# A hybrid decoder step on one core: the side loads of each head group issued by GpSimd's queue in place of SyncE's

## What is computed

```
for i in range(DEPTH):                                  # 2 layers
    h = rmsnorm(x, norm_pre)
    proj = h @ w_in                                     # 2048 -> 11296 columns, split among three branches
    y_ssd = ssd(...)     # depthwise conv4, chunked state scan with a carried state, gate, grouped norm
    y_att = swa(...)     # 128-wide sliding window attention, rotary keys, cached keys and values, sinks
    y_sc  = bg * conv3(cg * hh) * silu(g)
    x = x + rmsnorm(concat(y_ssd, y_att, y_sc) @ w_out, norm_post)
    x = x + sigmoid(x @ ple_gate) * (p[i] @ ple_proj)
# outputs: x, and per layer the conv tails, the ssd states, and the keys and values of the last 128 positions
```

## Time and profile before

| | |
|---|---|
| median of 3 runs | 2282.45 us (2279.03 to 2284.47) |
| the profiled execution | 2280.01 us, span 2278.1 us |
| PE busy | 2124.9 us, 93% |
| DVE busy | 1404.6 us, 62% |
| ACT busy | 1092.2 us, 48% |
| POOL busy | 53.8 us, 2% |
| transfers of SP and ACT (q1, q10) | 366.04 MB, 50.2% of 16 engines |
| transfers of POOL (q0) | 2.36 MB, 0.2% |
| mean granted clock of PE | 0.972 |

### The profile page before, as it was taken

How to read it: one execution, slowest core, us unless ns; L and a number is a source line. 1 busy time by engine, 2 the same in 40 slices (tenths; PEclk the granted TensorE clock), 3 DMA queues, 4 the chain that set the end, 5 groups by cost and what they waited for, 6 DMA issues and landing times.

```text
span 2278.1 us, 39608 instructions
## 1 busy us (share of the span) xinstructions
PE 2124.9 (93%) x15750; PEld 2059.2 (90%) x15750; DVE 1404.6 (62%) x2345; ACT 1092.2 (48%) x2151; POOL 53.8 (2%) x141
## 2 busy tenths in 40 slices
PE   4799999999999989998978999999999998999899
PEld 3799899899899989998967998998998997999899
DVE  4466767767766663437563666667667677534464
ACT  4456346446445443444443564564463465334443
POOL 0000000000001000000000000000000000000000
PEclk9899999999999999999988999999999999999999
DMA  5645545455365455543536455455454454555444
GB/s 174 185 140 178 161 163 175 147 181 178 118 204 169 134 179 177 176 160 123 164 131 180 140 168 192 139 170 194 142 176 156 168 177 135 173 183 175 136 141 151
DMA packets 146369, 370.94 MB, mean 163 GB/s; under 512 B 28584, under 2 KB 65256, under 8 KB 144744
## 3 DMA queue, kind: packets, MB, share of 16 engines
q1 hardware_dynamic: 133552, 336.39, 46.4%
q10 hardware_dynamic: 12488, 29.65, 3.8%
q0 software_dynamic: 144, 2.36, 0.2%
HBM read 340.41 MB, written 32.01 MB: 163 GB/s over the span
## 4 chain that ended last, share of the span: by engine, by line
PE 85%; DVE 7%; DVEq 3%; ACT 2%; issue 2%; DMA 1%; SPq 1%; ACTq 0%
PE main L426 25%; PE main L428 25%; PE main L427 24%; PE yo L545 2%; DVE wlo L1055 2%; PE yb L538 1%; DVE conv_sum L1262 1%; DVEq L1382 1%; ACT whi L723 1%; DVE work L1383 1%; PE yo L543 1%; PE t L619 1%; DVE mix L1421 1%; DVE y_or_x L1424 1%; DVEq L1422 0%
## 5 line engine op out<-in xcount | busy, mean ns | idle before, releaser
L426 PE MATMUL main<-h_hi,whi 128*128 128x288 f32 x4032 | 1223.7, 303 | 67.2 <-DVE h_lo L1055 21.7
L427 PE MATMUL main<-h_lo,whi 128*128 128x288 f32 x4032 | 1204.0, 299 | 0.0
L428 PE MATMUL main<-h_hi,wlo 128*128 128x288 f32 x4032 | 1199.9, 298 | 0.0
L1055 DVE TENSOR_TENSOR wlo<-raw,whi 128x1024 fp32r<-128x1024 f32 x568 | 690.8, 1222 | 491.9 <-ACT whi L723 478.9
L426 PEld LDWEIGHTS main<-h_hi,whi 128*128 128x128 f32 x4032 | 770.5, 191 | 87.8 <-issue 38.0
L427 PEld LDWEIGHTS main<-h_lo,whi 128*128 128x128 f32 x4032 | 772.3, 192 | 3.5 <-issue 1.9
L428 PEld LDWEIGHTS main<-h_hi,wlo 128*128 128x128 f32 x4032 | 773.2, 192 | 0.0
L723 ACT ACTIVATE whi<-raw 128x1024 fp32r<-128x1024 f32 x568 | 576.3, 1051 | 321.1 <-PE main L428 157.2
L1262 DVE SCALAR_TENSOR_TENSOR conv_sum<-conv_in,gpar_sb,conv_sum 128x312 f32<-128x312 f32 x144 | 90.1, 626 | 119.3 <-ACT conv_sum L872 111.3
L428 PE MATMUL main<-yssd_hi,wlo 128*128 128x288 f32 x512 | 152.5, 298 | 0.0
L426 PE MATMUL main<-yssd_hi,whi 128*128 128x288 f32 x512 | 151.2, 295 | 0.0
(11 more groups left out here) (239 smaller groups left out, 1702.8 us busy)
## 6 DMA issues: line engine op xcount, KB each, us to landing
raw<-wts SPq DMA_DIRECT2D x568, 512.0 KB, 3.7
work<-s_t SPq DMA_DIRECT2D x32, 512.0 KB, 5.9
ssm_s<-work ACTq DMA_DIRECT2D x8, 2048.0 KB, 7.2
work<-masks SPq DMA_DIRECT2D x8, 720.0 KB, 6.6
y_or_x<-xs SPq DMA_DIRECT2D x16, 288.0 KB, 4.2
xs<-y_or_x ACTq DMA_DIRECT2D x2, 2016.0 KB, 7.4
y_or_x<-x SPq DMA_DIRECT2D x4, 576.0 KB, 5.9
xs<-y_or_x POOLq DMA_DIRECT2D x1, 2304.0 KB, 7.8
```

The lines of the kernel that those rows point to most:

```text
L426: mm(out, w_hi, x_hi_, start=start, stop=False)
L427: mm(out, w_hi, x_lo_, start=False, stop=False)
L428: return mm(out, w_lo, x_hi_, start=False, stop=stop)
L1055: return tt(dst, raw, hi.bitcast(F32), ALU.subtract)
```

## The change

All of these side loads move from `@block.sync` to `@block.gpsimd`, with the same waits, the same order among themselves and the same semaphores. In POOL's program the first set stands at k = 0, the second at k = 1, and the four quarters of the old states at k = 14 to 17, which is behind `BM3` and ahead of the copies at k = 20. SP keeps the weights and the loads outside of the groups.

```
@@ @block.sync, for g, for k
                         load_unit(gunit(L, g, k))
-                        if k == 3:
-                            sp.wait_ge(smp_state, it(L, g))
...
-                            sp.dma_start(MSK, masks).then_inc(msk_in, 16)
-                        if k == 4:
-                            sp.wait_ge(ssd_done, it(L, g))
...
-                        if 15 <= k < 19:
...
@@ @block.gpsimd, for g, for k
+                        if k == 0:
+                            pool.wait_ge(smp_state, it(L, g))
+                            if L + g > 0:
+                                pool.wait_ge(y_sq, it(L, g - 1, 3, 2))
+                            pool.wait_ge(s1_stored, L * (G * 16) + g * 16 + 16)
+                            pool.wait_ge(k_stored, L * 32 + 32)
+                            pool.wait_ge(v_stored, L * 128 + 128)
+                            for r in range(2):
+                                pool.dma_start(KCUR[64 * r:64 * r + 64, :], kout[L, g]).then_inc(att_in, 16)
...
+                            pool.dma_start(VCUR[0:NSM, 2, :], v_g[NPR:T]).then_inc(att_in, 16)
+                            pool.dma_start(MSK, masks).then_inc(msk_in, 16)
+                        if k == 1:
+                            pool.wait_ge(ssd_done, it(L, g))
+                            pool.wait_ge(conv_saved, L * (G * 6) + g * 6 + 2)
...
+                        if 14 <= k < 18:
+                            i = k - 14
+                            if i == 0:
+                                pool.wait_ge(att_done, it(L, g))
+                            pool.dma_start(S0T...[:, :, i * P:(i + 1) * P], s0_t...).then_inc(st_in[i], 16)
                         if 8 <= k < 14:
```

More of the change, by code:

```diff
@@ L1487, in _ @@
                     for k in range(GRP_U):
+                        if k == 0:
[7 more added lines that the diff above has]
+                                pool.dma_start(KCUR[64 * r:64 * r + 64, :], kout[L, g]).then_inc(att_in, 16)
+                            pool.dma_start(KC[0:64, :], kc_t[L, g]).then_inc(att_in, 16)
+                            pool.dma_start(VC, vc_t[L, g].rearrange("w (b d) -> w b d", d=HD)).then_inc(att_in, 16)
+                            v_g = vout[L, g]
+                            pool.dma_start(VCUR[:, 0:2, :], v_g[0:NPR].rearrange("(c p) d -> p c d", p=P)).then_inc(att_in, 16)
+                            pool.dma_start(VCUR[0:NSM, 2, :], v_g[NPR:T]).then_inc(att_in, 16)
[3 more added lines that the diff above has]
+                            pool.wait_ge(conv_saved, L * (G * 6) + g * 6 + 2)
+                            pool.dma_start(GP[:, :], gpar[L, g]).then_inc(gp_in, 16)
+                            pool.dma_start(CSI[:, :], cs_in[L, g]).then_inc(sin_in, 16)
+                            pool.dma_start(SCI[:, :], sc_in[L, g]).then_inc(sin_in, 16)
+                        if 14 <= k < 18:
+                            i = k - 14
+                            if i == 0:
+                                pool.wait_ge(att_done, it(L, g))
+                            pool.dma_start(S0T.rearrange("p (b n) -> p b n", b=NB)[:, :, i * P:(i + 1) * P],
+                                         s0_t[L, g].rearrange("p (b n) -> p b n", b=NB)[:, :, i * P:(i + 1) * P]).then_inc(st_in[i], 16)
                         if 8 <= k < 14:
```

## The result

| | before | changed |
|---|---|---|
| median (4 runs each) | 2280.74 us (2278.86 to 2284.47) | 2323.07 us (2321.36 to 2330.38) |
| span of the profiled execution | 2278.1 us | 2321.1 us |
| PE busy | 2124.9 us | 2151.0 us |
| PE idle (span less busy) | 153.2 us | 170.1 us |
| span x (1 - granted clock) | 63.8 us | 88.2 us |

The change makes the kernel slower: the ratio is 1.0186, with a 95% interval of 1.0161 to 1.021. The forecast was faster, and the time is outside its range. The span grew by 43 us: 17 are idle time of PE, and the other 26 are busy time for the same 15750 matmuls, which fits the 24 us that the last row of the table gives to the clock (0.972 before, 0.962 now).

The account below looks back on a forecast made before the run. PE was taken as 93% busy, with 21.1 us winnable at two group-0 stalls. Gains of 8.6 + 4.2 = 12.8 us off 2280.0 gave 2267.2; with the median 2.4 us above the profiled execution, 2270 us, range 2261 to 2283.

Parts of the forecast that it names:

- What bounds the kernel now: PE 93% busy; two 8.0 us stalls ahead of group 0's first scores, 21.1 us with their low clock, the most winnable.
- The first set in group 0, issued by POOL: Six loads issued by 90.4, landing by 95 to 98, before PE's need at 100.20; both stalls go, 10.6 us each.
- Rival B: PE waits as long as before, POOL's issues being slow or late, or weights losing the gain: 2282 us; chance 0.21.
- What is late next: the halves of weights: After group 0's stalls, late weight halves take back 2 us in layer 0 and 6.4 us in layer 1.
- SP loses 13 issues per group: Fewer issues on SP, some 5 us for a run of seven, already covered by the weights' lead: 0 for groups 1 to 3.
- The first set in groups 1 to 3: POOL may issue from about 269.4, giving 19 us in place of 12 before PE's need: 0; 1 us a group for range.
- the second set: In group 0 only the first set is ahead of it, and it is read from unit 3 on: 0.
- The old states: Four quarters issued by POOL at 5.8 us each, landing 7 and 19 us before PE reads them: 0.
- The sum: Layer 0's 8.6 us plus layer 1's 4.2 us, 12.8 us off the profiled 2280.0, giving 2267.2, stated as 2270 us.
- Rival C: Slower: POOL writes the states' pieces too slowly, over 10.6 us a quarter; 2322 us at 12.3 us each; chance 0.12.

Follow-up runs that it names:

- x4: Kernel before, with only `vold` reshaped to four transfers of 16 rows, both copies at their old place; 2268.6 us, ratio 0.9923.
- x2: Kernel before, with `kold` and `vold` cut into a quarter per group behind units 6 and 7, `vold` in 16 rows; 2266.55 us, ratio 0.991.
- e2: Kernel before, with only the first and second sets moved to POOL, the old states staying on SP; 2285.74 us, ratio 1.0014.
- e1: Kernel before, with only the old states moved to POOL, the first and second sets staying on SP; 2315.3 us, ratio 1.0137.
- e3: Changed kernel, with each quarter of the states on POOL waiting for PE to finish a unit, at SP's former pace; 2286.29 us, ratio 1.0011.
- c2: Changed kernel, with POOL issuing the state quarters two and two, when PE has finished units 12 and 14; 2285.86 us, ratio 1.002.
- e4: Kernel before, with SP issuing all four quarters of the states back to back at k = 15; 2340.0 us, ratio 1.0252.
- x1: Kernel before, with ACT issuing both copies, `kold` and `vold`, unchanged but later, behind unit 6 of group 0; 2283.44 us, ratio 0.9985.
- f1: Kernel before, with ACT making the second half's high part behind the decays at units 14 to 17; 2282.47 us, ratio 0.9997.
- c4: Changed kernel, with POOL's whole burst of states issued earlier, behind the copies of unit 12; 2298.84 us, ratio 1.0076.
- f2: Changed kernel, with the same ACT order as f1 at units 14 to 17; 2298.13 us, ratio 1.0061.

## Why the prediction was wrong

- **What bounds the kernel now:** right. The stall's cause was read correctly from q10's share: x4 changes nothing but the shape of `vold`'s transfers, and the stall is all but gone. Its price was right too: 21.1 us foretold for both with their clock, 21.2 won by x2.
- ***The first set in group 0, issued by POOL*** failed, and with it the 12.8 us of the sum. The issues were right (the last of six by 90.4 foretold, 89.10 + 0.54 measured). The landing, "by 95 to 98", was not: 107.5. I held the stretch of small pieces to be free for another queue because the load "has a queue of its own"; but nothing on it moved until these pieces were nearly through, and then it met the large packets, which it was to run ahead of. The row said as much: q10's share was 121% in that stretch. Rival B, with 0.21, had this outcome for the stall, and the load among the large packets; its slow or late issues did not come. e2, at 2285.7 us, is this part by itself; B's 2282 was for it.
- ***What is late next: the halves of weights*** was not put to the test, as there was no gain to be late behind. ACT got the half of the step at 103.41 in place of 101.07, 2.3 us later, where the step counted some 2; whether PE would have stood for it no run shows. PE's waits for `wlo` grew from 4.8 to 6.7 us over the span, the longest of them is 4.4 as before.
- ***SP loses 13 issues per group***: they are 14 (7, 3 and 4), and no part of the sum hung on it. ***The first set in groups 1 to 3*** and ***the second set***: right, nothing (e2: no new wait of PE there).
- ***The old states*** failed, and this made the result. I set their own landing against their own reader and found 7 and 19 us of cover; that PE never waits for a quarter was right. But the step asked only about the transfer that was moved, and not about the stream that it was moved beside. SP's order had two halves of weights between quarters. POOL's has none. The half that ACT takes ahead of the decays was kept back by 3 us, and the decays have less slack than the weights themselves. PE's row for waits on weights gave the wrong comfort here: it shows the slack of PE behind weights, and not of what ACT has queued behind them.
- ***The sum*** has 0 for the states, and so has the range: its 1 us a group stood for the first set. The term is 4 us a group: 32 us in e1 over 8 groups, more than half of it clock, and 42 us with the other part. The low clock was priced only behind the stall that was to go, and nowhere as something that a new pause of 1 us could bring.
- **Rival C** has the sign and even the number (2322 against 2323), but not the mechanism, so it is no success. POOL is quick with the pieces: 922 ns for a quarter (the changed kernel, groups of POOL: count, busy us and mean ns), and 5.5 us to its landing in e3. That is far from the 10.6 us from which C decides, and the issue is 6 times quicker than the 5.8 us of the proportional price.

```profile
L1486 POOL DMA_DIRECT2D work<-s_t x32 | 29.3, 922 | 0.0
```

By the Trainium skill's rule on shared engines ("DMA: Bandwidth & Descriptors", "Issuing engines are not separate DMA queues") another issuer saves only the time of issuing. The runs that keep the pace agree in their times: e2, e3 and c2 stand within 4 us of before, and a quarter lands in 5.5 us from POOL and in 5.9 from SP. The 2282 us of the prediction would have held for them (e3: 2286.3, with 2283.1 for before). The change itself is 42 us off, since its queue also set anew when the transfers *begin*; a quarter lands in 9.2 us there. The first set lands later from POOL in each of these runs too, the masks in 12.1 to 12.6 us in place of 6.6. It starts there beside the store of the last group's states (from 272 to 278 us of the changed kernel q10 had 91 to 115%), and PE does not wait for it from group 1 on. The other rule weighed, DVE locking GpSimd out of its port ("SBUF — State Buffer", "Who interferes with whom"), left no mark: all 32 quarters were issued in 0.88 to 1.02 us, those of group 1 while DVE was busy for 3.9 of 4 us. Whether DVE ran a form there that takes the lock no run shows.

## What to carry to other kernels

A hand-written order in one queue does two things: it says which engine pays for the issue, and it spreads the transfers in time. Whoever moves a load to a free queue keeps only the first and must put the pace back by a wait (e3), or the bytes start at once and push back the stream beside them. The question is then not only who reads the moved load, but who reads the stream in order, and what else that engine has queued behind; e4 and x1 show the same link at two other places. And before a queue is blamed for a slow small transfer, look at what large or badly shaped transfers run beside it: one reshaped DRAM to DRAM copy (x4) gave what ten issues on another queue could not.

## What the runs showed of the hardware

- A copy from DRAM to DRAM whose slowest dimension is 4 went in packets of 62 KB, some 3 to 5 engines at a time (a share of 20 to 29%), and an 8 KB load beside it took 17.1 us on SP's queue and 18.4 on POOL's; with 16 rows, 7.8 us on SP's.
- Beside a copy in small pieces (1177 packets in 3 us, share 121%) SP's queue moved nothing from 88 to 91 us before the change. In the changed kernel POOL's queue stood still for nearly 5 us beside it, from the issue at 86.3 to about 91, while SP's got a share of 12 to 54%.
- POOL issued 512 KB in 1024 pieces in 0.92 us, and its packets held several pieces: 559 packets for 2.04 MB (some 4000 pieces of 512 bytes) on q0, where SP's queue took 1593 packets for 2.33 MB of weights and states.
- In all 8 groups of the changed kernel a pause of PE of 0.7 to 1.4 us was followed by 4 us or more at the lower clock, 1.7 us lost for each 4. The clock's share of the loss (24 us) is larger than that of all idle time (17 us). Such stretches come also with PE busy for 6 us ahead of them (none in the profile of before, three in f1, five in the changed kernel and in e3); what brings those is unexplained, and so is why the clock's loss differs by 14 us between runs of c4 and by 21 between runs of f2.
